# A diffusion-transformer layer on eight cores: masks on VectorE, another order of the experts, and a final sum that is split between TensorE and VectorE

## What is computed

```
def rmsnorm(x, g):
    inv = lax.rsqrt(jnp.mean(x * x, axis=-1, keepdims=True) + NORM_EPS)
    return x * inv * g

hc = modulate(rmsnorm(ctx, norm1_g), csh1, csc1);  k_ctx, v_ctx = context_kv(hc, w_in)
h  = modulate(rmsnorm(x, norm1_g), sh1, sc1)
b, cg, xin, q, k, v, ga, gb = split_in(h @ w_in)
ya = (b * (b_conv + sum(up[:, j:j + L] * w_conv[j] for j in range(3)))) @ w_a   # up: cg * xin, padded
yb = window_attention(rope(q), rope(k), v, k_ctx, v_ctx, sink) @ w_b    # keys with |q - k| <= 128, and all context
x  = x + g1 * (sigmoid(ga) * ya + sigmoid(gb) * yb) @ w_o

h = modulate(rmsnorm(x, norm2_g), sh2, sc2)
# top-1 group of 4, then the top-2 of its 8 experts; gates combine[:, e] for 32 experts
y = sum(combine[:, e:e + 1] * ((silu(a_e) * u_e) @ w_down[e]))   # a_e, u_e = split(h @ w_up[e])
return rmsnorm(x + g2 * y, final_g)
```

## Time and profile before

| what | us |
|---|---|
| median of 3 executions (903.32 to 922.6) | 905.18 |
| the profiled execution, device time | 906.63 |
| its span on the slowest core (core 2) | 904.7 |
| spans of the eight cores | 882.5 to 904.7 |
| PE busy / DVE / ACT / POOL in the span | 751.6 / 532.2 / 379.1 / 327.2 |

### The profile page before, as it was taken

How to read it: one execution, slowest core, us unless ns; L and a number is a source line. 1 busy time by engine, 2 the same in 40 slices (tenths; PEclk the granted TensorE clock), 3 DMA queues, 4 the chain that set the end, 5 groups by cost and what they waited for, 6 DMA issues and landing times. The chain is left out here.

```text
span 904.7 us, 14299 instructions; the slowest of 8 cores (882.5 to 904.7 us)
## 1 busy us (share of the span) xinstructions
PE 751.6 (83%) x5494; PEld 422.5 (47%) x5494; DVE 532.2 (59%) x1054; ACT 379.1 (42%) x687; POOL 327.2 (36%) x383
## 2 busy tenths in 40 slices
PE   6887799898999999999999943899699959788461
PEld 2344455343455444454444422576476637556210
DVE  1548946799743656568698787644344334333197
ACT  2326422644466775424253341045245415344353
POOL 2021411335344754211211104267577637632200
PEclk9988999999999999999999965799899979989685
DMA  8994799999977899999988899379989999996498
GB/s 151 209 204 152 153 147 155 150 149 126 149 108 105 187 158 174 196 151 173 188 138 136 128 180 165 97 223 304 223 264 213 229 220 248 245 234 216 153 323 321
DMA packets 37007, 168.41 MB, mean 186 GB/s; under 512 B 11692, under 2 KB 13868, under 8 KB 28611
## 3 DMA queue, kind: packets, MB, share of 16 engines
q0 software_dynamic: 27136, 140.36, 80.6%
q1 hardware_dynamic: 9796, 27.06, 8.8%
HBM read 234.26 MB, written 58.72 MB: 324 GB/s over the span
## 5 line engine op out<-in xcount | busy, mean ns | idle before, releaser
L550 PE MATMUL ps<-sb 128*128 128x512 bf16 (+10 forms) x4452 | 685.8, 310 | 116.5 <-DVE sb L583 24.8
L550 PEld LDWEIGHTS ps<-sb 128*128 128x128 bf16 (+4 forms) x4452 | 361.9, 102 | 416.0 <-issue 79.1
L563 ACT ACTIVATE sb<-ps 128x512 bf16<-128x512 f32 (+4 forms) x385 | 211.2, 588 | 339.5 <-PE ps L550 247.6
L568 DVE TENSOR_TENSOR sb<-ps,sb 128x256 bf16<-128x256 f32 (+4 forms) x196 | 85.4, 446 | 159.3 <-PE ps L550 79.9
L563 ACT ACTIVATE sb<-ps,sb 128x512 bf16<-128x512 f32 x136 | 83.4, 687 | 53.1 <-PE ps L550 29.9
L1350 POOL DMA_INDIRECT sb<-hd,sb x68 | 74.7, 1098 | 77.3 <-PE ps L1362 49.6
L580 DVE SCALAR_TENSOR_TENSOR sb<-sb 128x1024 f32<-128x1024 f32 (+4 forms) x96 | 101.5, 1072 | 1.5
L1401 POOL DMA_INDIRECT yd<-sb x68 | 72.9, 1072 | 55.0 <-ACT sb L563 34.3
L565 ACT ACTIVATE sb<-sb 128x1024 bf16<-128x1024 f32 x50 | 52.8, 1055 | 89.6 <-DVE sb L568 56.1
L898 POOL TENSOR_TENSOR sb<-sb 128x512 bf16<-128x512 bf16 x60 | 66.7, 1121 | 61.4 <-ACT sb L563 61.0
L1381 DVE TENSOR_TENSOR sb<-sb 128x2048 bf16<-128x2048 bf16 x34 | 41.7, 1226 | 76.0 <-DMA sb<-wex 43.2
(11 more groups left out here) (52 smaller groups left out, 246.5 us busy)
## 6 DMA issues: line engine op xcount, KB each, us to landing
wbf<-wex POOLq DMA_DIRECT2D x72, 384.0 KB, 12.4
sb<-wbf POOLq DMA_DIRECT2D x18, 1536.0 KB
sb<-wex POOLq DMA_DIRECT2D x16, 1536.0 KB
sb<-wad POOLq DMA_DIRECT2D x12, 1024.0 KB, 21.2
sb<-x SPq DMA_DIRECT2D x16, 512.0 KB, 23.1
sb<-wsl POOLq DMA_DIRECT2D x8, 1024.0 KB, 32.6
sb<-x POOLq DMA_DIRECT2D x16, 512.0 KB, 12.4
sb<-yd SPq DMA_DIRECT2D x16, 512.0 KB, 12.8
```

The source lines that it names most:

```text
L550: ins = e.matmul(o, lhsT=l, rhs=r, start=s0, stop=s1)
L563: S.op("act", lambda e: e.activation(out=out, in_=in_, func=func, scale=scale), reads=[in_] + list(extra), writes=w)
L568: S.op(eng, lambda e: e.tensor_tensor(out=out, in0=a, in1=b, op=op), reads=[a, b], writes=[out])
```

## The change

1. **Masks.** The 60 mask products go from POOL to DVE. The first tap of the convolution (`ts`, 16 times) goes from DVE to ACT. The shift of every third norm-1 tile goes from POOL to DVE. ACT copies three of four transposed norm-1 tiles instead of one of two.
2. **Loads and prefetch.** The x tiles from the seventh on, and the context tiles, are loaded through POOL's queue. The prefetch begins once tile 8 has been loaded, with one step per tile in norm 1. 19 experts are converted (76 steps), and `PREK`, the steps per later stage, goes from (14, 16, 16, 16, 10) to (10, 16, 16, 16, 8).
3. **Order of the experts.** Those whose number is not 7 modulo 8 come first, with the overflow blocks at the same places; 7, 15, 23 and 31 come last. Of those behind the first six, two of every three are converted, and the last four too: in the expert stretch 9 loads are float32 (two of them overflow blocks) and 19 bf16, where there were 10 and 18.
4. **Two halves of `yd`.** A token's row is now token + 2048·(half), and a sign flip puts rows of experts 7 modulo 8 always in half 1. So half 0 is complete four items before the end. Token labels are interleaved to fit.
5. **The last item** (expert 31) isn't scattered. Zero rows are scattered early in its place (`Z`), its results stay in SBUF (`YLt`), and one-hot matrices `PL` (two DVE operations of 128 x 2048 at items 6 and 7) let PE add them in the final sum. The first three loads of half 0 start before the end of the items; SP's loads no longer wait for the branch and the join. `Dn` of items 31 and 32 stands before the next `U`, `Dn(33)` behind the branch.
6. **Final sum.** Per half tile PE now runs four bf16 matmuls (two halves of `yd`, two one-hot ones). For tiles 1, 4, 7, 10 and 13 a float32 identity matmul adds the residual too; DVE's add is dropped there, ACT squares from PSUM, and DVE scales from PSUM in two halves.
7. **Scheduler.** Its model now lets a DVE operation with two SBUF operands wait for POOL, and follows reads and writes apart for the skipped regions. Routing gains three small DVE operations per chunk.

The core of the diff:

```
-            sdma(xs[t % 6], src, ("xs", t % 6), also=[("xl", t)])
+            if t < 6:
+                sdma(xs[t % 6], src, ("xs", t % 6), also=[("xl", t)])
+            else:
+                gdma(xs[t % 6], src, ("xsg", t % 6), also=[("xl", t)])
...
-            tt(xn[t % 2], x_, mod1[:, 2 * c, :], ALU.add, eng="pool" if t % 3 == 2 else "dve")
+            tt(xn[t % 2], x_, mod1[:, 2 * c, :], ALU.add)
...
-            weave(main, [(1.0, n1_step(t)) for t in nxt])
+            n1s = []
+            for t in nxt:
+                n1s.append((1.0, n1_step(t)))
+                if t >= XC:
+                    n1s.append((0.0, pre_step))
+            weave(main, n1s)
...
-                ts(t_, UC[:, j, o0:o0 + 512], wcs[:, j * 3:j * 3 + 1], bcs[:, j:j + 1], ALU.mult, ALU.add, rd=[wcs, bcs])
+                S.op("act", lambda e: e.activation(out=t_, in_=u_, func=AF.Identity, bias=bcs[:, j:j + 1], scale=wcs[:, j * 3:j * 3 + 1]),
...
-                        S.op("pool", lambda e, p4=p4, m_=m_: e.tensor_tensor(out=p4, in0=p4, in1=m_.unsqueeze(1).to_broadcast([128, 4, 128]), op=ALU.mult),
+                        S.op("dve", lambda e, p4=p4, m_=m_: e.tensor_tensor(out=p4, in0=p4, in1=m_.unsqueeze(1).to_broadcast([128, 4, 128]), op=ALU.mult),
...
+        two = eng == "dve" and sum(1 for k, c in rd if k is None and len(c) >= 64) >= 2
...
+                if o["two"]:
+                    ce += max(0.0, st["pb"] - t)
...
             for h in range(2):
                 b_ = bank("main")
-                mm(b_[:], [(b_[:], identb, y_[:, k_, h * 512:(h + 1) * 512], k_ == 0, k_ == 1) for k_ in range(2)], [identb, y_])
+                xl = [(q4(b_[:]), identf, xv, False, False)] if t in wide else []
+                mm(b_[:], [(b_[:], identb, ya, True, False), (b_[:], identb, yb, False, False)] + xl
+                   + [(b_[:], PL[s][:, q, k_, :], YLt[s][:, hs], False, s == 1) for s in range(2)],
...
+                if xl:
+                    act(junk2[t % 2][:, hs], b_[:], AF.Square, accum=s3h[:, h:h + 1])
+                    hb.append(b_)
+                else:
+                    tt(xv, xv, q4(b_[:]), ALU.add)
```

More of the change, by code:

```diff
@@ L110, in op @@
             wr.append(self._where(a))
[L111 to L134, removed]
-        deps.discard(-1)
[L136 to L144, removed]
-        for k, c in wr:
-            if k is None:
-                self.lw[c] = oid
-            else:
-                self.res[k] = [oid, []]
+        for tr in self.trackers:
+            tr.deps(deps, rd, wr)
+        deps.discard(-1)
+        two = eng == "dve" and sum(1 for k, c in rd if k is None and len(c) >= 64) >= 2
+        self.ops.append(dict(two=two, eng=eng, fn=fn, deps=deps, dma=dma, sig=False, cost=self._cost(eng, writes, dma, cost, fast)))
+        for tr in self.trackers:
+            tr.note(oid, rd, wr)
         return oid
@@ L178, in _run @@
         n = len(ids)
+        if st is not None:
+            st["out"] = []
         succ = {i: [] for i in ids}
@@ L252, in _run @@
                 heapq.heappush(ev, (at[i], 0, i))
+        keep = None
         while len(out) < n or any(rings[r][0] for r in rings):
+            if len(out) == n and keep is None:
+                keep = (tprev, {r: [list(q) for q in rings[r][0]] for r in rings})
             nd = next_dma(tprev)
@@ L283, in _run @@
         assert len(out) == n
+        if keep is not None:
+            tprev = keep[0]
+            for r in rings:
+                rings[r][0] = keep[1][r]
         st["t"] = tprev
@@ L628, in pre_step @@
             o_ = wbf_d[q, p * 32:(p + 1) * 32, :]; i_ = wex_d[prel[q], p * 32:(p + 1) * 32, :]
[L629 removed]
+            S.op("pool", lambda e: e.dma_start(out=o_, in_=i_), reads=[("wbf", h - PRED)] if h >= PRED else [("xl", XC)], writes=[("wbf", h)], dma=("wbf", h % PRED), cost=PREC)
         def mix(lst, k):
@@ L1046, in n2_steps @@
             return out
-        items = [("s", e_) for e_ in range(NE)]
+        items = [("s", e_) for e_ in stat_e]
         for k_ in range(KDYN):
             items.insert(12 + k_ * 20 // KDYN, ("d", k_))
+        items += [("s", e_) for e_ in last_e]
         NA = len(items)
@@ L1403, in O @@
                     in_=YB[q], in_offset=None, bounds_check=2 * L - 1, oob_is_err=False),
-                    reads=[YB[q], ix], writes=[("yd", i, s)], dma=("YB", q), cost=0.8 if items[i][0] == "s" else 0.05)
+                    reads=[YB[q], ix] + ([("yl", q_, b_) for q_, b_ in yord] if i >= NA else []), writes=[("yd", i, s)], dma=("YB", q), cost=0.8 if items[i][0] == "s" else 0.05)
         G(0)
@@ L1422, in run_items @@
                     f_()
-                if i > lo:
+                if i > lo and i - 1 not in early and i != NA:
                     Dn(i - 1)
```

228 lines of the change are left out of this document (172 added, 56 removed).

## The result

The changed kernel is slower by 1.7%: a ratio of 1.0167 to before, with a 95% interval of 1.0142 to 1.0193, about 15 us. The forecast was 871 us, a ratio of 0.963, and a range that ended at 893.

A forecast was written before the change was run, and what follows sets the result against it. PE rarely waits in long stages; weights pace the experts, DVE limits the final sum. −6 − 4 − 22 + 7 − 4.5 − 5 = −34.5 on 906.63 gives 872.1, against the median 871 us; 8-in-10 range 847 to 893.

The forecast's parts named there:

- Term A: Norm 1 and projections: adds moved to DVE close PE's gaps, free DMA covers seven more prefetch steps; −6 us.
- Term B: Attention: masks on DVE shrink from 1.12 to 0.42 us and part of PE's idle 10.3 us is won; −4 us.
- C: Routing to experts: gathers no longer behind two weight loads, so U(0) starts at 555 to 558 instead of 579; −22 us.
- overflow: Overflow work, now in items 2 to 5 of the experts, is only partly covered by PE's waiting for weights; +7 us.
- D: Pace of the experts: one float32 weight load becomes bf16 while the queue sets the pace; −4.5 us.
- Term E: Final sum: less DVE work and less waiting for the last scatters, partly lost to PE and DVE waiting mutually; −5 us.
- The first: Rival, final sum: PE at the slow clock becomes the bound, +24 us, time 900; chance 0.09.
- The second: Rival, attention: masks wait in DVE's list, making attention 60 us longer, time 935; chance 0.06.
- The third: Rival, start of the experts: the earlier start is worth 0 in place of −15, time 886; chance 0.12.

The follow-up runs named there:

- e10: e7 with the 60 masks back on POOL: ratio 0.9716 to the kernel before.
- e7: Changed kernel, prefetch step's scheduler price 4.1, W(4) and W(5) behind the first gathers, first DVE overflow operation waiting for the first transposed tokens: ratio 0.9733, median 882.1 us.
- e18: Kernel before with only the scheduler's price of a prefetch step lowered from 4.1 to 3.3: ratio 1.0325.
- e6: Changed kernel with only the scheduler's price of a prefetch step put back from 3.3 to 4.1: ratio 0.9909.
- e8: Kernel before with only W(4) and W(5) behind the first gathers and overflow operations behind the first transposed tokens: ratio 0.9855.
- e9: e7 with no tile of the final sum summed whole on PE, all 16 residual adds on DVE: ratio 0.9763.
- e16: Changed kernel with the scheduler's price of a wo load raised from 1.5 to 6.0, prefetch price left at 3.3: ratio 1.0057.
- e11: Changed kernel with only the eight wo loads moved from POOL's queue to SP's, price left at 3.3: ratio 1.0200.
- e13: e7 with the wo loads moved to SP's queue as well: ratio 0.9938.

## Why the prediction was wrong

**Term A (−6), nearly right.** The last transposes of norm 1 start at 132.6 instead of 137.3, a gain of 4.8, and the gaps at 72 and 105 us are gone; what remains is 3.37 us at 79. DMA went to 1.01 there, above the 0.9 that the prediction named. The count of seven more steps holds: ten lie ahead of 130 us, where three lay.

**Term B (−4), wrong, and with it the prediction.** The last score product of attention comes at 373.8 instead of 353.2. With the 4.8 us that A had won by the first one (155.1 instead of 159.9), attention is 25.4 us longer. PE is idle in 29.8 us of it instead of 10.3, of which 9.6 are waits for `wad` (7.00 and 2.63) and 12.26 the wait behind DVE's operation on `wo`; and it is busy 5.9 us longer, at a granted clock of 0.94 instead of 1.00. The parts of the term were sized well; the groups by form after:

```profile
L947 DVE TENSOR_TENSOR sb<-sb 128x512 bf16<-128x512 bf16 x60 | 24.3, 414 | 3.6 <-ACT sb L600 3.1
L617 DVE SCALAR_TENSOR_TENSOR sb<-sb 128x512 f32<-128x512 bf16 x32 | 23.5, 748 | 2.3 <-ACT sb L897 2.0
```

A mask takes 414 ns (424 forecast), and the taps fell from 1001 to 748 ns, which gives 8.1 us back (10.2 forecast). That the masks' move wins anything isn't shown, since e10 with them on POOL can't be told from e7. The step that failed is the one sentence "The prefetch has the same number of steps here or fewer, four more in all, which lie in A." The number was nearly right, 39 steps instead of 36 between those two score products, and the conclusion wrong: the steps' number says little of their place between the loads in POOL's list. That place comes from the scheduler's price. The diff lowers it from 4.1 to 3.3, the list of the change ahead of the prediction leaves that out, and the prediction put it at nothing. It compared the two orders of POOL's list at the start of the experts and not in attention, where 34 steps instead of 28 now stand between the sixth and the seventh wad load. (Ahead of the first wo load it is only 17 instead of 16, so that count alone can't be the cause.) e18 shows that this edit alone costs the kernel before 28 us, e6 that undoing it alone wins 43 us up to routing. The bound of +4.6 for B was a bound on DVE's load, and it held: DVE is busy 128.2 us between those two score products instead of 131.2. What was missing is a bound on waiting.

**The end of attention to routing (forecast 0), wrong by the same cause.** This part is 15 us longer, and e6, with the old price alone, has its routing product back at 529.16. The row at 423.71 with 6.51 us for `wad` is the largest single piece; the others are small and I could not put each to a cause.

**Terms C, overflow and D (−22 + 7 − 4.5 = −19.5), nearly right.** Measured −15.6. U(0) starts at 594.09, 22.0 us behind the routing product instead of 42.4, so C is −20.4; from there to the last transposes it takes 4.7 us more than before, where the overflow work and D were forecast at +2.5.

```profile
594.09 3.66 PE L587 MATMUL ps<-sb 128*128 128x256 bf16 x32
```

e8 has the same mechanism alone, in the kernel before, at 0.9855. That the stream of weights carries the gain through to the end also holds: DMA is at 0.96 in the experts instead of 0.91. But that the order came out this way is luck of the scheduler. e6 lost it by the price alone. And the kernel before has it too with nothing but the lower price: in e18 U(0) starts 18.2 us behind the routing product at 579.91.

```profile
598.16 3.66 PE L550 MATMUL ps<-sb 128*128 128x256 bf16 x32
```

So at 3.3 the gain here and the loss in attention come with the same edit, and the prediction counted the gain alone.

**Term E (−5), the right sign, and its size in part luck.** On the two slowest cores the last part is 5.2 us shorter, but over all eight cores the mean falls only from 69.9 to 67.2. The float32 tiles are some 1.5 us of that, by e9 against e7. DVE's adds and scalings fell to 35.5 us, as forecast (35.9). PE's products were underpriced: the 24 records of the earlier trace rows are of 12 products, since the code has one in each of eight sums and four for the norm's gain, so one product there took 16.0 / 12 = 1.33 us and not 0.783. Measured are 10.2 us for ten, where the prediction had 7.8.

**The rivals.** The first, PE at the slow clock in the final sum, didn't happen: the granted clock there is 0.92, up from 0.67, with PE busy 46.6 of 65.0 us instead of 24.4 of 63.7. The Trainium skill, page "TensorE: Matmul & The Clock Gate", section "HAM oscillation — how this bites in real kernels", has waits between bursts as the cause of the slow clock; the pair, 0.67 with more waiting and 0.92 with less, agrees. The second had the right picture, DVE's ordered list holding attention up, with the wrong cause: masks on DVE cost nothing measurable once the queue is in order (e7 against e10), but everything on DVE waits behind one operation whose weights are late. The third didn't happen in the changed kernel, but it did in e6, where U(0) comes 55 us behind the routing product.

**What stays open.** The price carries the loss, but not every microsecond of it has an owner. e16 wins about 10 us back, but it moves the other loads as well as DVE's operations on `wo`; e11 shows that changing the queue of those loads doesn't win anything. How much is the wait for `wo`, how much the waits for `wad`, and what follows from them in the order, wasn't separated. Nor is it known why 4.1 is so good; only four prices were tried.

## What to carry to other kernels

A number in a build-time scheduler's cost model is an edit to every queue. Before costing a change, compare the new order of each in-order list around the loads that someone waits for, in every stage, not only at the place where the change looks large. Where an order matters, write it as a dependence (e7), since a scheduler's order can come out the other way with the next change. And on an engine that holds urgent work, an operation on late data costs the wait of everything behind it, not its own microsecond.

## What the runs showed of the hardware that I had not expected

- A float32 identity product of 128 x 512 stands in the trace as two records of 591 ns each, ten products 10.2 us, at a granted clock of 0.95. The group by form in e7's final sum (busy us, mean ns):

```profile
L587 PE MATMUL ps<-sb 128*128 128x512 f32 x20 | 10.2, 591 | 0.0
```

  The Trainium skill, page "FP8 and Floating Point Precision", section "TensorE Precision Notes", says that true FP32 takes four passes through the array. By that an estimate is 4 × 0.226 = 0.90 us for a product; 1.02 was measured.
- Another queue was no way past a crowd of transfers: moved to SP's queue the same 512 KB loads had a median of 19.7 us to landing (e13) instead of 13.3 on POOL's (e7), beside the same prefetch on POOL's queue.
